# A third seven-product unit, the second of eight, in the 1024-column group of the mixer's output projection

## What is computed

```python
D_MODEL = 2048
SEQ = 256
...
    merged = jax.nn.sigmoid(m_a) * (y_a @ w_proj_a) + jax.nn.sigmoid(m_b) * (y_b @ w_proj_b)
    return merged @ w_out
```

## Time and profile before

| | us |
|---|---|
| median of 3 runs | 2039.89 (2039.8 to 2040.57) |
| profiled execution | 2040.56 |
| its span, first to last instruction | 2038.5 |
| TensorE busy | 2029.9 |
| VectorE busy | 1589.4 |
| ScalarE busy | 1028.4 |

### The profile page before, as it was taken

The page is one execution under the profiler, slowest core; times in us unless marked ns, Lnnn a source line. Parts: engine busy times, 40 slices in busy tenths (PEclk is TensorE's granted clock), DMA queues, the critical chain, the costliest instruction groups (busy, mean ns, idle before and its releaser), DMA issues.

```text
span 2038.5 us, 25810 instructions
## 1 busy us (share of the span) xinstructions
PE 2029.9 (100%) x10324; PEld 1728.8 (85%) x10324; DVE 1589.4 (78%) x1949; ACT 1028.4 (50%) x1029; POOL 16.0 (1%) x34
## 2 busy tenths in 40 slices
PE   9999999999999999999999999999999999999999
PEld 7888888888888888888888888888888888888887
DVE  5778586779775777678988987888886778987776
ACT  6555353455654555565545554454554434444642
POOL 0000000000000000000000000000000000000000
PEclk9999999999999999999999999999999999999999
DMA  9666656446566675465655666565567554554462
GB/s 328 215 200 206 186 182 213 168 159 206 185 210 229 232 258 190 152 215 166 207 195 183 201 206 200 173 206 181 190 213 243 185 179 140 191 172 151 139 248 104
DMA packets 255335, 397.95 MB, mean 195 GB/s; under 512 B 18944, under 2 KB 166448, under 8 KB 253552
## 3 DMA queue, kind: packets, MB, share of 16 engines
q1 hardware_dynamic: 251088, 375.28, 56.0%
q0 software_dynamic: 3408, 18.92, 2.5%
q10 hardware_dynamic: 720, 2.11, 0.3%
HBM read 392.09 MB, written 4.19 MB: 194 GB/s over the span
## 4 chain that ended last, share of the span: by engine, by line
PE 93%; DVE 2%; DMA 2%; ACT 1%; issue 1%; SPq 0%; DVEq 0%; ACTq 0%
PE ps L747 85%; PE pm L747 7%; DMA raw<-in_w_in 2%; PE pm L750 1%; DVE wl L1956 1%; ACT wh L1339 1%; DVE cv L1964 0%; DVE ybT L1964 0%; DVE vs L1956 0%; DVE up L2141 0%; DVE uT L2141 0%; ACT junk L1359 0%; DVE xt L1964 0%; ACT L1339 0%; ACT cv L1339 0%
## 5 line engine op out<-in xcount | busy, mean ns | idle before, releaser
L1956 DVE TENSOR_TENSOR wl<-raw,wh 128x2048 fp32r<-128x2048 f32 (+2 forms) x384 | 781.6, 2054 | 194.6 <-ACT wh L1339 149.4
L1339 ACT ACTIVATE wh<-raw 128x2048 fp32r<-128x2048 f32 (+1 forms) x357 | 664.3, 1874 | 331.8 <-PE ps L747 275.1
L747 PE MATMUL ps<-xt,wh 128*128 128x512 f32 (+2 forms) x2224 | 518.3, 389 | 0.3 <-ACT wh L1339 0.2
L747 PEld LDWEIGHTS ps<-xt,wh 128*128 128x128 f32 (+1 forms) x2224 | 410.2, 188 | 82.9 <-ACT wh L1339 0.7
L747 PE MATMUL ps<-wh,xt 128*128 128x512 f32 x1888 | 459.4, 391 | 1.4 <-ACT wh L1339 1.3
L747 PEld LDWEIGHTS ps<-wh,xt 128*128 128x128 f32 x1888 | 351.9, 188 | 75.1 <-issue 1.5
L747 PEld LDWEIGHTS ps<-xt,wl 128*128 128x128 f32 x2192 | 272.8, 192 | 5.7
L747 PE MATMUL ps<-xt,wl 128*128 128x256 f32 x2192 | 274.7, 283 | 0.0
L747 PE MATMUL ps<-wl,xt 128*128 128x512 f32 x944 | 242.2, 389 | 0.4 <-DVE wl L1956 0.4
L747 PEld LDWEIGHTS ps<-wl,xt 128*128 128x128 f32 x944 | 176.9, 188 | 38.2 <-DVE wl L1956 1.6
L1339 ACT ACTIVATE cv<-up,vt 128x256 f32<-128x256 f32 x88 | 52.5, 601 | 221.1 <-DVE up L1956 221.1
(11 more groups left out here) (512 smaller groups left out, 1868.4 us busy)
## 6 DMA issues: line engine op xcount, KB each, us to landing
raw<-in_w_in SPq DMA_DIRECT2D x146, 1024.0 KB, 5.1
raw<-in_ffn_w_up SPq DMA_DIRECT2D x84, 1024.0 KB, 5.2
raw<-in_ffn_w_down SPq DMA_DIRECT2D x43, 1024.0 KB, 5.1
raw<-in_w_out SPq DMA_DIRECT2D x32, 1024.0 KB, 5.1
raw<-in_w_proj_b SPq DMA_DIRECT2D x16, 1024.0 KB, 5.1
raw<-in_w_proj_a SPq DMA_DIRECT2D x8, 1024.0 KB, 5.2
raw<-in_xa_wk SPq DMA_DIRECT2D x4, 1024.0 KB, 5.8
raw<-in_xa_wq SPq DMA_DIRECT2D x4, 1024.0 KB, 5.1
```

The source lines that it names most:

```text
L747: return p.matmul(out, l, r, start=start, stop=stop, skip_group_check=share)
L1339: return a.activation(out, in_, func, bias=bias, scale=scale)
L1956: return v.tensor_tensor(out, a, b, op)
```

## The change

PAIRS gives for each kind of activation the units that are seven-product units. For "mg" unit 1 is added to 3 and 5, so that ww0 has three of them. The sums for unit 1 need the k chunks 2 and 3, from mg_turn0. They become mg_forms0 at slot (pb2, 3); the sums of unit 3 are now mg_forms1 and stay at (pb3, 0.5), those of unit 5 are mg_forms2 and stay at (pb3, 3).

```diff
-    ("pb1", 2): ["mg_turn0"], ("pb2", 2): ["mg_turn1"], ("pb3", 2): ["mg_turn2"], ("pb3", 0.5): ["mg_forms0"], ("pb3", 3): ["mg_forms1"], ("ww0", 1): ["mg_turn3"], ("ww0", 6): ["ww0_sums"],
+    ("pb1", 2): ["mg_turn0"], ("pb2", 2): ["mg_turn1"], ("pb3", 2): ["mg_turn2"], ("pb2", 3): ["mg_forms0"], ("pb3", 0.5): ["mg_forms1"], ("pb3", 3): ["mg_forms2"], ("ww0", 1): ["mg_turn3"], ("ww0", 6): ["ww0_sums"],
...
-PAIRS = {"h1": (1, 3, 5), "mg": (3, 5), "ac": SEVEN}
+PAIRS = {"h1": (1, 3, 5), "mg": (1, 3, 5), "ac": SEVEN}
...
-            "mg_forms0": lambda: mg_forms(0), "mg_forms1": lambda: mg_forms(1), "ww0_sums": lambda: dw_sums("ww0"),
+            "mg_forms0": lambda: mg_forms(0), "mg_forms1": lambda: mg_forms(1), "mg_forms2": lambda: mg_forms(2), "ww0_sums": lambda: dw_sums("ww0"),
```

## The result

The changed kernel takes 2046.67 us (median of 7 runs, 2045.44 to 2047.16) against 2039.89 before (7 runs): 6.78 us slower, ratio 1.0032, 95% interval 1.0022 to 1.0043. The forecast was 2044.05 with a range to 2046.4: the direction was right, the size too small.

A forecast was written before the change was run, and what follows sets the result against it. TensorE's matmul stream was taken as the bound. To the 2039.89 us median came stall 4.77 and restart 0.17, less 0.67 saved and 0.1 already paid: +4.16, giving 2044.05 us, range 2043.0 to 2046.4.

The forecast's parts named there:

- The bound: Whole kernel: TensorE's stream of matmuls bounds it, no single wait exceeds 1.1 us, and any standstill adds in full.
- What is removed: Unit ww0,1 goes from 24 to 21 matmuls of 512 columns, saving 0.67 us.
- what is added before pb3: mg_forms0 at (pb2, 3) delays VectorE's low split of pb3,1 by about 1.4 us; under cover, costed at nothing.
- The stall: Start of ww0,1: TensorE waits 4.77 us, from 691.70 to 696.47, for banks that mg_turn3 filled.
- The sum without the clock: At ww0,1: stall 4.77 and restart 0.17, less 0.67 saved and 0.1 already paid, gives +4.16 us.
- The clock: Behind the stall at ww0,1: no fall in the likeliest case; if it falls to 1.2 GHz, 1.6 us more.
- a third of the unit, 1.6 us: Extra time taken for ww0,1 in the case in which the clock falls behind the stall.
- The first rival: Clock falls behind the stall before ww0,1: +5.8 us, 2045.7, at the most 8.9; chance 0.36.
- the whole of ww0,1 once more: Upper end of the cost if the clock falls to 1.2 GHz behind the stall: 4.76 us.
- The banks are free in time: Rival at ww0,1: mg_turn3's low parts finish by 691.6, leaving the bare saving, −0.67 us, 2039.2; chance 0.04.
- A shorter stall: Rival at ww0,1: ScalarE reaches mg_turn3's copies earlier, stall 2.47 us, +1.9 us, 2041.8; chance 0.08 with part given back.
- The stall is longer: Rival at ww0,1: wl of ww0,2 pushes VectorE's first low part; each 0.1 us counts; within main case's spread, chance 0.52.

The follow-up runs named there:

- mg_turn3 in the middle of ww0,0: Changed kernel with mg_turn3 between ww0,0's token blocks on TensorE and ahead of ww0,1's differences on VectorE and ScalarE: 2039.10 us, again 2039.04.
- filled kernel: Changed kernel with 19 idle 512-column matmuls on TensorE ahead of the wait for all four banks: 2043.92 us; with 7 instead of 19: 2045.71 us.
- mg_turn3 first: Changed kernel with VectorE and ScalarE taking mg_turn3 one split earlier, TensorE's order unchanged: 2043.69 us.
- the first kernel of the plain unit: Kernel before, with only a TensorE wait ahead of plain unit ww0,1 for mg_turn3's last low part: 2042.33 us.

## Why the prediction was partly wrong

**The bound** was read rightly: TensorE's stream is the bound, and what it stood still was added in full (the stretch from ww0 to ww0,2 is 7.21 us longer, the span 6.9). Its list of TensorE's waits left out three smaller ones (1.0, 0.5 and 0.4 us), which stand in both traces and change nothing.

**What is removed, and what is added before pb3.** The sums cost nothing, as forecast: VectorE's low split of pb3,1 starts about 1.3 us later (658.61, with the 0.4 us of the whole program 659.01, for 657.73) and TensorE doesn't notice. The saving was forecast at 0.67; with mg_turn3 in the middle of ww0,0 the trace shows 0.46, as ww0,1 took 4.95 us and not 4.76.

**The stall.** The chain up to VectorE's last low part held to a few hundredths. That 4.74 us were measured for 4.77 is in part luck. The prediction counted from the moment at which the next matmul could have started (691.70), the trace counts idle time from the modelled end of the transposes; counted as the prediction did, the stall is 4.99 us (696.29 less 691.30, the start of the transposes plus 0.79). The missing 0.2 us is the handover: 0.10 us was read from TensorE to VectorE, and was used for the other way, where it is 0.36 us here, as in the filled kernels and the one with mg_turn3 first. Why it is longer there was not asked; in the first kernel of the plain unit it is 0.06 (693.49 to 693.55). The kernel with mg_turn3 first (2.96 us) and the one with it in the middle (none) show that the two queues and the two banks are its cause. The sum without the clock was +4.16; the filled kernel shows +4.06 between the medians and +4.34 in the stretch, so the sum was right to 0.2 us.

**The clock.** Here the prediction failed, in two terms. The step "I take none of it for the likeliest case, since every row reads 1.00" drew on a trace whose longest gap was 1.1 us, and so said nothing on one of 4.8. The row of slices, taken for "no slice below 1.00", couldn't even have shown a fall: it reads the same after the change. All seven runs of the changed kernel lost clock (0.998 or 0.999). And "a third of the unit, 1.6 us" for the case in which it falls was too small: 3.0 us in the profiled execution, 2.75 between the medians with and without the gap filled. The first rival, whose mechanism was right, gave 2045.7, and the range, built around it, ended 0.3 us below the median. By its own bound, the whole of ww0,1 once more (4.76 us), the range should have reached further. The prediction gave the Trainium skill's warning ("TensorE: Matmul & The Clock Gate", section "Why this matters for your kernels") that a gap between bursts can put the clock back; the runs agree with it: the clock fell in most executions at a gap of 2.96 us and in all at 3.16 us and longer.

**The other rivals.** "The banks are free in time" did not happen, but it names the remedy: with the banks freed at 690.2 the stall and the fall are gone. "A shorter stall" did not happen either; nothing was given back later. "The stall is longer" did, by 0.2 us, but through the handover and not through VectorE's queue.

## What to carry to other kernels

A unit that starts an accumulation in spare banks inherits the wait of whoever used them last; ask which stage filled them just before, and where its emptying stands in the other engines' queues. Here a stall of 4.7 us on TensorE, which was otherwise never idle for long, cost itself and 2.75 us of slow restart on top. A trace without such a gap is no evidence that the clock will hold, and a clock averaged over 51 us doesn't show a fall of 7 us; read it from narrow windows behind the gap. The remedy is cheap here: put the small stage inside the unit ahead, so that its emptying is hidden. Even so the third seven-product unit then saves less than can be told from no change.

## What the runs showed of the hardware

How the clock behaved behind a gap, at this one place, with the length of the gap from each kernel's profiled execution: 2.18 us, one of ten executions read below 1.00; 2.96 us, seven of ten; 3.16, 3.91, 4.74 and 5.05 us, all (six, six, seven and six runs). These means over the span have three decimals, so a stretch of less than 2 us at half clock can hide in a 1.000, and the small counts are lower bounds. The price did not grow with the gap: in the profiled executions ww0,1 lost 1.7 us behind 3.16 and 5.05 us, 2.8 us behind 3.91 us and 3.0 us behind 4.74. In the traces it is half of the time at 1.2 GHz behind the restart: 3.4 us for the two cheap ones, 5.7 and 6.2 us for the others. It also varies between executions of one kernel (2045.44 to 2047.16 for the change, where the filled kernel varies by 0.7 us). What decides how long the clock stays low was not settled. I had not expected that useless matmuls in a gap can pay: here 19 of them gave back 2.75 us.
